# Cross-attention in a two-block network on one Trainium2 core: when ScalarE rounds the second output matrix, and where it loads the exponential's table

## The reference, cut to what matters

```python
def cross_attention(h, mem_n, wq, wk, wv, wo):
    q = (h @ wq).reshape(bsz, seq, X_HEADS, X_HEAD_DIM)      # 4 heads of 256
    k = (mem_n @ wk).reshape(bsz, m_len, X_HEADS, X_HEAD_DIM)
    v = (mem_n @ wv).reshape(bsz, m_len, X_HEADS, X_HEAD_DIM)
    s = jnp.einsum('bqhd,bkhd->bhqk', q, k) * (X_HEAD_DIM ** -0.5)
    p = jax.nn.softmax(s, axis=-1)
    o = jnp.einsum('bhqk,bkhd->bqhd', p, v).reshape(bsz, seq, D_MODEL)
    return o @ wo

x = x + cross_attention(rms_norm(x, norm_x_g), rms_norm(mem, norm_mem_g), w_xq, w_xk, w_xv, w_xo)
x = x + hierarchical_moe(rms_norm(x, norm_ffn_g), ...)
```

## Time and profile before

| | |
|---|---|
| median of three executions | 1499.16 us |
| the profiled execution, its own time | 1498.63 us |
| its span, first to last instruction | 1496.8 us |
| PE busy | 1355.4 us (91%) |
| DVE busy | 535.8 us (36%) |
| ACT busy | 414.1 us (28%) |
| POOL busy | 390.8 us (26%) |
| mean granted TensorE clock | 0.957 |

### The profile page before, as it was taken

How to read it: one execution, slowest core, us unless ns; L and a number is a source line. 1 busy time by engine, 2 the same in 40 slices (tenths; PEclk the granted TensorE clock), 3 DMA queues, 4 the chain that set the end, 5 groups by cost and what they waited for, 6 DMA issues and landing times. The chain is left out here.

```text
span 1496.8 us, 16779 instructions
## 1 busy us (share of the span) xinstructions
PE 1355.4 (91%) x6344; PEld 901.3 (60%) x6344; DVE 535.8 (36%) x1074; ACT 414.1 (28%) x809; POOL 390.8 (26%) x372
## 2 busy tenths in 40 slices
PE   6998998999799889987878878886999999999899
PEld 5776775898658733332322322325888887788467
DVE  3649757430062511111111111117321414563753
ACT  5333366164331100000000000015323224343641
POOL 7553223168410011111111111110344450000321
PEclk9999998999999799999999999998999999999899
DMA  7221131254204879999999999984232322222000
GB/s 208 77 94 56 57 113 49 89 172 141 84 5 182 355 298 370 422 421 423 421 422 422 423 424 422 421 349 144 85 113 85 105 93 85 85 85 85 29 22 36
DMA packets 72369, 298.27 MB, mean 199 GB/s; under 512 B 10169, under 2 KB 10217, under 8 KB 51569
## 3 DMA queue, kind: packets, MB, share of 16 engines
q1 hardware_dynamic: 64848, 282.80, 48.2%
q0 software_dynamic: 7456, 14.59, 3.0%
HBM read 293.16 MB, written 12.58 MB: 204 GB/s over the span
## 5 line engine op out<-in xcount | busy, mean ns | idle before, releaser
L747 POOL TENSOR_TENSOR ring_rounded<-ring,ring_rounded 128x512 fp32r<-128x512 f32 x192 | 253.2, 1355 | 341.1 <-ACT ring_rounded L1462 341.1
L874 PE MATMUL bank<-HT_rounded,ring_rounded 128*128 128x512 f32 (+1 forms) x576 | 221.2, 384 | 3.4 <-DVE ring_rounded L2355 2.0
L876 PE MATMUL bank<-HT_rounded,ring_rounded 128*128 128x512 f32 (+1 forms) x576 | 217.7, 378 | 0.0
L875 PE MATMUL bank<-ring_rounded 128*128 128x512 f32 (+1 forms) x576 | 217.7, 378 | 0.0
L1175 PE MATMUL bank<-ring,B 128*64 128x512 f32 x704 | 180.8, 667 | 34.4 <-DMA ring<-in_w 33.5
L1175 PEld LDWEIGHTS bank<-ring,B 128*64 128x64 f32 x704 | 55.0, 152 | 144.2 <-issue 112.6
L2247 DVE TENSOR_TENSOR B<-bank,small 128x512 f32<-128x512 f32 x32 | 22.1, 692 | 326.5 <-PE bank L1165 326.5
L876 PE MATMUL bank<-ring_rounded 128*128 128x512 f32 x352 | 138.1, 392 | 0.0
L1462 ACT ACTIVATE ring_rounded<-ring 128x2048 fp32r<-128x2048 f32 x54 | 102.8, 1916 | 110.6 <-DMA ring<-in_w_in_a 46.6
L874 PEld LDWEIGHTS bank<-HT_rounded,ring_rounded 128*128 128x128 f32 x576 | 108.5, 188 | 30.7 <-issue 6.4
L875 PEld LDWEIGHTS bank<-ring_rounded 128*128 128x128 f32 x576 | 108.4, 188 | 20.3 <-issue 1.0
(11 more groups left out here) (381 smaller groups left out, 1999.2 us busy)
## 6 DMA issues: line engine op xcount, KB each, us to landing
ring<-in_w SPq DMA_DIRECT2D x88, 1024.0 KB, 30.2
A<-in_w SPq DMA_DIRECT2D x21, 2048.0 KB, 28.8
ring<-in_w SPq DMA_DIRECT2D x11, 2048.0 KB, 28.6
XN<-in_w SPq DMA_DIRECT2D x20, 1024.0 KB, 29.1
HT<-in_w SPq DMA_DIRECT2D x20, 1024.0 KB, 32.2
ring<-in_w_in_a SPq DMA_DIRECT2D x16, 1024.0 KB, 5.0
ring<-in_w_in SPq DMA_DIRECT2D x14, 1024.0 KB, 7.3
ring<-in_w_in_b SPq DMA_DIRECT2D x8, 1024.0 KB, 5.4
```

What stands on the lines that cost most here:

```text
L747: last = pool.tensor_tensor(r32(lo), lo, r32_read(quarter(g, True)[:, k, :]), ALU.subtract)
L874: pe.matmul(o, r32(a_hi), r32(b_hi), start=first, stop=False)
L875: pe.matmul(o, r32(a_hi), r32(b_lo), start=False, stop=False)
L876: return pe.matmul(o, r32(a_lo), r32(b_hi), start=False, stop=last)
```

## The change

Two things move on ScalarE. The table load of the exponential goes to the middle of the query copies: a one-column exponential of a constant (its result is used by nothing) is put behind the high parts of `xw0`, and the table load goes with it. The two halves of `xw1` go from ahead of the loop to inside it: half 0 ahead of the exponential of step 4, half 1 ahead of that of step 8.

```diff
             for m in range(8):
                 if m == 4:
                     high_parts("xw0")
+                    act.activation(root[:, 79:80], ms[:, 79:80], ACT.Exp)
                 o = filled(U["xq", m])
                 act.activation(xqT[:, m, :], o[:, :], ACT.Copy, scale=1.0 / 16).then_inc(done, 1)
-            high_parts("xw1")
             for i in range(16 + 4):
+                if i in (4, 8):
+                    high_half("xw1", i // 8)
                 if i < 16:
                     o = filled(U["xs", i])
                     act.wait_ge(sem("xmax_ready"), i + 1)
```

## The result

The changed kernel took 1488.02 us, median of five executions (1483.27 to 1491.23), against 1498.93 for the kernel before in the same series (1494.87 to 1501.07). The ratio is 0.9925, with a 95% interval of 0.9905 to 0.9945: 11 us or 0.75% faster, where 6.9 us and at least 1490.0 us had been forecast. The direction was right, the size and the range were not. The profiled execution of the changed kernel took 1489.01 us; its span is 1487.2 us, its mean granted clock 0.964 (0.957 before), PE is busy for 1347.6 us (1355.4 before), ACT for 414.2 (414.1).

What follows compares the result with a forecast made beforehand. ScalarE's queue holds up the cross-attention loop's start, and TensorE waits for the loop. 7.4 + 1.1 - 0.9 - 0.7 = 6.9 us gained gives a median of 1492.3, taken as 1492.0; range 1490.0 to 1495.4 us.

Steps and rivals of the forecast that it cites:

- Term 1: Loop start: exponential 0 comes right behind the first row maximum, so TensorE's first transposes start earlier; 7.4 us gained.
- Term 2: First transposes to exponential 3: without the long stand TensorE's clock stays full; 1.1 us gained.
- The table load at nothing: Query copies: the moved load of 1.28 us fits a 6.67 us ScalarE gap, so it costs nothing.
- Terms 3 and 4: Halves in steps 4 and 8: late exponentials and slow scales beside GpSimd delay TensorE; 0.9 and 0.7 us lost.
- the first and the third: Loop clock rivals: it falls for a while, 1494.1 us, chance 0.08; it stays low throughout, 1520 us, chance 0.03.
- The table was not loaded again: Rival: a copy before the loop brings other tables, forcing a reload before exponential 0; 1493.3 us, chance 0.02.
- Nothing was given back behind the loop: Rival: the expert stage, paced by its weights, gives the gain back; time stays at 1498.6 us, chance 0.06.
- The lock at half a us: Scales 4 and 8 beside GpSimd's subtractions: each was taken to lose 0.5 us.
- the upper bound, 0.93 us for one scale: Most a scale beside GpSimd was seen to lose: a mixer scale took 1.28 us, 0.93 above 0.35.
- the whole subtraction of 1.24 us: By the skill's lock rule a scale could lose a whole subtraction; two would lose 2.5 us, leaving 5.4 gained.
- The bounds: The forecast's own limits from the two scales beside GpSimd, +1.0 and -0.9 us: 1491.0 to 1493.2 us.
- Runs of one kernel spread by up to 2 us upward: Whole executions: scatter assumed when setting the range, cited from 1501.07 against 1499.16 us.

Runs made afterwards that it cites:

- before + 16 dummies: The kernel before, with 16 dummy matmuls run by TensorE while it waits ahead of the loop's first transposes; ratio 0.9976 to before, mean 1494.9 us.
- low parts behind the last transposes: The changed kernel, with GpSimd making the low parts of xw1 after the loop's last transposes; ratio 0.9946 to before, mean 1490.5 us.
- halves behind the loop: The changed kernel, with ScalarE rounding both halves of xw1 after the loop; run twice, ratios 0.9913 and 0.9924 to before, mean 1486.4 us.
- low parts ahead of the router's loads: The changed kernel, with GpSimd making xw1's low parts after the last score tile, before the router's loads; ratio 0.9949 to before, mean 1490.7 us.
- low parts behind score tile 15: The changed kernel, with GpSimd making xw1's low parts after the last score tile and the router's loads; ratio 0.9998 to before, mean 1498.2 us.

## Why the prediction was wrong where it was, and right where it was

Each step of the loop, counted from the start of the last query copy:

| step | before | forecast | measured | before + 16 dummies | low parts behind the last transposes | halves behind the loop |
|---|---|---|---|---|---|---|
| first transposes | 10.14 | 2.7 | 2.76 | 10.08 | 2.75 | 2.76 |
| exponential 3 | 13.06 | 4.6 | 4.59 | 12.06 | 4.58 | 4.59 |
| transposes of tile 4 | 16.44 | 8.8 | 8.59 | 15.07 | 8.13 | 7.44 |
| transposes of tile 8 | 25.19 | 18.3 | 17.75 | 23.81 | 16.87 | 16.17 |
| first matmul with xw0 | 44.36 | 37.5 | 36.92 | 42.98 | 36.04 | 35.34 |

- *Term 1, the first exponential.* 7.4 us were forecast and 7.38 measured.
- *Term 2, the clock.* Up to exponential 3 it is 1.09 us (8.47 less 7.38), as forecast. But exponential 3 started at 414.38 before, and the clock came back only just after 415: the cost didn't end where the term stopped counting. From exponential 3 to the transposes of tile 4 it took 3.38 us before, 3.01 with the 16 dummy matmuls and 2.85 with the halves behind the loop. Without any half in the loop, terms 1 and 2 are 44.36 - 35.34 = 9.02 us and not 8.5, so term 2 stood for 1.6 us and not 1.1. The run with 16 dummy matmuls shows 1.38 us of it as the clock alone; the other 0.3 would fit the scales of tiles 1 and 2, which GpSimd's subtractions made slow in that run (0.84 and 0.51 us for 0.35) and which the term left out. It is not one number either: with six traces of the kernel before the clock costs 1.3 to 2.1 us, by where in the stand it falls and when it comes back.
- *The table load at nothing.* Right; 5.14 us of the gap are left. Its share of the gain is 1.2 us, since without the move it waits for the row maximum and then runs on the path.
- *Terms 3 and 4, the two halves.* Set against the run with both halves behind the loop, half 0 costs 8.59 - 7.44 = 1.15 us (0.9 forecast) and half 1 costs 9.16 - 8.73 = 0.43 us from the transposes of tile 4 to those of tile 8 (0.7 forecast). The mechanism was right in both parts. The delay of the exponential is read from the run with the low parts behind the last transposes: 0.69 us for half 0 and 0.01 for half 1 (0.4 and 0.2 forecast). The slow scale beside GpSimd (0.80 and 0.77 us for 0.35) adds 0.46 and 0.42 (0.5 each forecast). That the sum of the two terms is 1.58 us as forecast (1.6) is luck: the two errors in the slack cancel.
- *The rivals.* The clock stayed at 1.00 through the loop, in spite of 32 transposes and two stands of about 1 us, against the first and the third. Longer stands do bring the first about: in the run with the low parts ahead of the router's loads the clock fell after 1.99 and 0.85 us. The table was not loaded again. Nothing was given back behind the loop.
- *The lock at half a us.* Right for this kernel. But the upper bound, 0.93 us for one scale, was too low as a bound on what this mechanism can do: the same instruction stood for 9.73 us in the run with the low parts behind score tile 15, and so was the whole subtraction of 1.24 us that the prediction weighed beside it.
- *The bounds.* "1491.0 to 1493.2" counts its lower end from 1492.0 and its upper one from 1492.3; from one value it is 1491.0 to 1492.9. Nothing hangs on it.

**The steps that failed** are two. In the sum it is term 2, which was mis-sized: the cold matmuls were counted only up to exponential 3, at 1.1 us, and the term came out at 1.6 (1.38 of it shown as the clock's). With the other terms as they came out, the loop gained 7.44 us, or 7.6 against the mean of six traces, and not 6.9. In the range it is "Runs of one kernel spread by up to 2 us upward". That was read off three executions. Over 96 executions of the kernel before the standard deviation is 3.0 us, from 1490.5 to 1505.1, and it works in both directions. A median of five of them is good to about 3 us, and a range with its lower end 2 us under the forecast could not hold it.

The sum's 1492.3 us lie 4.2 us above the measured 1488.02. Of these, 0.5 are the starting point (1499.16 against the mean of 1498.7), 0.7 the size of the gain in the loop, and 1.3 the luck of five executions, since over 17 the changed kernel is at 1489.3 us. The remaining 1.7 us are the difference between the gain in the means, 9.4 us with an uncertainty of 1.6, and the 7.6 that the traces show in the loop. They are hardly more than the uncertainty; no trace shows them in any stretch, an excess of that size stands in kernels with a longer loop too, and its cause stays open. Term 2 alone would not have put the time outside the range (1499.16 - 7.44 = 1491.7).

## What to carry to other kernels

Work that is needed late should not stand between two stages in an in-order queue: look for the first later gap in which both its own engine and the engine it feeds are idle, here behind the loop, and not for any place that is merely past the start. When the stall that is removed has cooled TensorE down, add the cold matmuls behind it to what it costs, up to the row in which the clock is back and not to the next convenient mark, and as a span and not as one number. And take the scatter of whole executions from many of them before a range is set; a gain of half a percent is read better from a stretch of the trace that repeats to 0.01 us (36.91 to 36.92 here) than from medians.

## What the runs showed of the hardware that was not expected

- A VectorE scale beside back-to-back GpSimd subtractions usually waits for the end of one (0.50 to 1.47 us in place of 0.35), but in one place was shut out for all eight (9.73 us). Which of the two happens was not settled.
- GpSimd slows a scale when it only issues a DMA, too: scale 14 takes 0.74 us in the traces in which the first of the router's loads (0.92 us of GpSimd) is issued beside it (here load at 428.32, scale at 428.59), before and after the change, and 0.35 us with the halves behind the loop, where that load comes later.
- A table load runs behind the wait of the activation that it belongs to: it started 0.77 us after ScalarE was free, when the row maximum came. It took 1.28 us and the activation followed at once (398.61, then 399.90). The Trainium skill (ScalarE: Activation LUTs, section "What ACT_TABLE_LOAD costs") adds a drain of 1.38 us to each switch; no such gap is in these rows, nor ahead of the load in the earlier trace rows (ScalarE free at 408.35, load at 408.37).
- Programs that differ up to there by no more than a table load in a gap reached their last query copy between 396.48 and 405.86 us in these traces, and one place where they differ is how long the clock stays low after a stand (0.50 against 0.77 in the window from 140 above).
